# A hybrid MLA / mLSTM / MoE step on one core: w_o and x of the output stage loaded one stage earlier, into other rooms

## The reference, cut to what matters

```python
xp = layer_norm(ALPHA_RES * xp + gp1 * mixer_out(o_p, h_p, mo_p, p), p['ln1_g'], p['ln1_b'])   # mixer_out ends in @ w_o
xs = layer_norm(ALPHA_RES * xs + gs1 * mixer_out(o_s, h_s, mo_s, p), p['ln1_g'], p['ln1_b'])
u2 = concatenate([xp * (1 + scp2) + shp2, xs * (1 + scs2) + shs2])
logits = u2 @ router_w + router_b            # top 4 of 32 experts, softmax over the 4
f = moe(u2)                                  # w_up (32, 1024, 2048), w_down (32, 1024, 1024)
xp, xs = layer_norm(ALPHA_RES * x + g2 * f)  # ln2
```

## Time and profile before

| what | value |
|---|---|
| median of 3 runs (lowest, highest) | 2225.05 us (2221.8, 2225.31) |
| the profiled execution: time / span in the trace | 2224.97 us / 2223.1 us |
| PE busy, share of the span | 1879.3 us, 85% |
| decode attention (508.0 to 664.3 us) | 156.3 us, PE busy 142.10, DMA 39 GB/s |
| output and router (664.3 to 821.4 us) | 157.1 us, PE busy 119.17, DMA 212 GB/s |
| experts (821.4 to 2151.0 us) | 1329.6 us, PE busy 1127.29, DMA 319 GB/s |
| combine (2151.0 to 2223.0 us) | 72.0 us, PE busy 50.67, DMA 182 GB/s |

### The profile page before, as it was taken

One profiled execution on the slowest core, in us unless ns is written; L12 is line 12 of the kernel. 1 busy time (PEld: TensorE's weight loads), 2 busy tenths in 40 slices (PEclk: granted clock), 3 DMA queues, 4 the chain that ended last, 5 costly groups with the idle time before them and its releaser, 6 DMA issues. The chain is left out here.

```text
span 2223.1 us, 52280 instructions
## 1 busy us (share of the span) xinstructions
PE 1879.3 (85%) x21217; PEld 1085.7 (49%) x21218; DVE 606.0 (27%) x1916; ACT 443.0 (20%) x1005; POOL 206.9 (9%) x277
## 2 busy tenths in 40 slices
PE   4999897988986959999758998497797969999947
PEld 2546485566563545555324554153354535555523
DVE  2412255163332552222101221021121212222215
ACT  0102112322210012222211222021122212222210
POOL 0000101100001200011000110000000000110125
PEclk9998958898987969999978999698899979999978
DMA  9342114400309178089999089999989996651884
GB/s 361 136 154 86 47 57 159 137 1 24 85 6 290 57 307 354 24 334 409 404 402 385 24 331 410 402 402 409 401 310 403 402 410 251 241 231 42 344 317 155
DMA packets 170208, 539.49 MB, mean 243 GB/s; under 512 B 26202, under 2 KB 75550, under 8 KB 137396
## 3 DMA queue, kind: packets, MB, share of 16 engines
q1 hardware_dynamic: 143744, 502.33, 58.8%
q0 software_dynamic: 7392, 22.81, 3.0%
q10 hardware_dynamic: 19028, 13.77, 2.1%
HBM read 504.73 MB, written 33.99 MB: 242 GB/s over the span
## 5 line engine op out<-in xcount | busy, mean ns | idle before, releaser
L1697 PE MATMUL psum<-arena 128*32 128x256 f32 x11904 | 733.0, 399 | 151.3 <-DMA arena<-in_w_up 131.3
L1697 PEld LDWEIGHTS psum<-arena 128*32 128x32 f32 x11904 | 392.8, 115 | 446.5 <-DMA arena<-in_w_up 158.9
L1706 PE MATMUL psum<-arena 128*32 128x256 f32 x5952 | 357.5, 381 | 30.3 <-DMA arena<-in_w_down 15.8
L1749 DVE TENSOR_TENSOR arena<-psum,arena 128x256 f32<-128x256 f32 x186 | 79.0, 425 | 1017.0 <-PE psum L1697 1017.0
L1706 PEld LDWEIGHTS psum<-arena 128*32 128x32 f32 x5952 | 187.4, 110 | 161.0 <-issue 23.2
L1670 ACT ACT_TABLE_LOAD x93 | 119.3, 1283 | 211.6 <-issue 211.6
L1670 ACT ACTIVATE arena<-arena 128x128 f32<-128x128 f32 x186 | 57.7, 310 | 380.1 <-DVE arena L1753 380.0
L406 PE MATMUL psum<-arena 128*128 128x512 f32 (+2 forms) x400 | 128.6, 480 | 0.0
L1641 POOL COPY arena<-arena 128x1 uint32 (+1 forms) x94 | 17.0, 181 | 1133.6 <-PE psum L1687 1114.1
L1672 ACT ACTIVATE arena<-psum 128x128 f32<-128x128 f32 x186 | 51.6, 277 | 246.0 <-PE psum L1692 246.0
L406 PEld LDWEIGHTS psum<-arena 128*128 128x128 f32 x400 | 70.6, 209 | 58.0 <-issue 58.0
(11 more groups left out here) (347 smaller groups left out, 1666.8 us busy)
## 6 DMA issues: line engine op xcount, KB each, us to landing
arena<-in_w_up SPq DMA_DIRECT2D x128, 2048.0 KB, 20.7
arena<-in_w_down SPq DMA_DIRECT2D x64, 2048.0 KB, 29.8
arena<-in_w_ada SPq DMA_DIRECT2D x10, 2048.0 KB, 17.5
d_y<-arena ACTq DMA_DIRECT2D x372, 32.0 KB, 5.2
arena<-in_w_in SPq DMA_DIRECT2D x5, 2048.0 KB, 8.1
d_y<-arena SPq DMA_DIRECT2D x1, 10240.0 KB, 33.1
arena<-in_cache_ckv SPq DMA_DIRECT2D x8, 1024.0 KB, 5.7
arena<-in_b_up SPq DMA_DIRECT2D x128, 64.0 KB, 13.1
```

Source lines behind the costliest of these rows:

```text
L1697: ins = pe.matmul(bank[c * U:(c + 1) * U, 0:256].rearrange("p (g n) -> p g n", g=2), xT[:, 2 * q + k, :], up[par][q][:, k, :, c * 256 + h ...
L1706: ins = pe.matmul(Y[c * U:(c + 1) * U, 0:256], hidT[:, h, n * U:(n + 1) * U], down[par][h][:, n, c * 256:(c + 1) * 256], start=(h == 0 and ...
L1749: dve.tensor_tensor(pre, bank[:, 0:256].rearrange("p (g n) -> p g n", g=2), bu[par][:, :, h * P:(h + 1) * P], ALU.add).then_inc(s["h_sum"], 1)
```

## The change

In the decode attention stage SP gets four more DMAs, behind the eight of the new keys and ahead of the caches: w_o's first half, its second half (after `new_in`, the landing of the new keys), and x in two parts (after `ql_acc` and `ql_out`, when the latent queries are done). w_o goes to column 3000 and x to 15064, which nothing uses any more then. The output stage takes both from there and no longer loads them. The rooms left free there take u2 and x1 (36076, 38124); `tmp`, two buffers for the gated product in norm, becomes one, `tm`, at 51436. The first four rooms of `RING_AT[0]` change their order. Expert 0's w_up piece 0 is still loaded at once, piece 1 now after all transposes of the mixed rows (`mT_acc`), pieces 2 and 3 after the last project as before. The last four loads of the stage (w_down of expert 0, two pieces of expert 1) now stand behind the waits for the stores of x1 and u2 and for the transposes of u2 (`uT2_acc`). The instructions of PE, DVE, ACT and POOL and their waits are the same.

```diff
-RING_AT = [[3000, 7096, 27576, 31672, 35768, 39864], [43960, 48056, 11192, 15288, 19384, 23480]]
+RING_AT = [[31672, 27576, 3000, 7096, 35768, 39864], [43960, 48056, 11192, 15288, 19384, 23480]]
...
+    v.wo, v.x_in = v.cut(3000, 2, KD, 512), v.cut(15064, NT, D)
...
+            w_o = I["w_o"][0]
+            sp.dma_start(v.wo[:, 0], w_o[:, 0:512].rearrange("(k p) n -> p k n", p=P)).then_inc(s["wo_in"], 16)
+            sp.wait_ge(s["new_in"], 16 * B)
+            sp.dma_start(v.wo[:, 1], w_o[:, 512:].rearrange("(k p) n -> p k n", p=P)).then_inc(s["wo_in"], 16)
+            sp.wait_ge(s["ql_acc"], 2 * H)
+            sp.wait_ge(s["ql_out"], 2 * H + 1)
+            sp.dma_start(v.x_in[:, 0:NP_T, :], I["x_prompt"][0].rearrange("(t p) d -> p t d", p=P)
+                         ).then_inc(s["x2_in"], 16)
+            sp.dma_start(v.x_in[:, NP_T, :], I["x_sample"].rearrange("b t d -> (b t) d")).then_inc(s["x2_in"], 16)
             sp.wait_ge(s["yz_out"], 16)
...
-    wo = v.cut(27884, 2, KD, 512)
-    x = v.cut(36076, NT, D)
+    wo, x = v.wo, v.x_in
...
-    u2 = v.cut(15064, 2, D)
-    x1 = v.cut(17112, 2, D)
-    tmp = v.cut(19160, 2, D)
+    u2 = v.cut(36076, 2, D)
+    x1 = v.cut(38124, 2, D)
+    tm = v.cut(51436, D)
...
-            for q in range(2):
+            def first(q):
                 sp.dma_start(v.cut(RING_AT[0][q], 2, 2 * FF), first_up(0, q)).then_inc(s["ring_in"][q], 16)
-            for t in range(NT):
+
+            first(0)
+            for t in range(NT):
+                if t == NT - 2:
+                    sp.wait_ge(s["mT_acc"], 2 * NT)
+                    first(1)
                 if t == NT - 1:
                     sp.wait_ge(s["wo_acc"], NT)
-                    for q in range(2, 4):
-                        sp.dma_start(v.cut(RING_AT[0][q], 2, 2 * FF), first_up(0, q)).then_inc(s["ring_in"][q], 16)
+                    first(2)
+                    first(3)
...
+            for par, n in ((0, (NT + 1) // 2), (1, NT // 2)):
+                sp.wait_ge(s["x1_out"][par], 16 * n)
+                sp.wait_ge(s["u2_out"][par], 16 * n)
+            sp.wait_ge(s["uT2_acc"], 2 * NT)
             for h in range(2):
                 sp.dma_start(v.cut(RING_AT[0][4 + h], 4, D), first_down(0, h)).then_inc(s["ring_in"][4 + h], 16)
```

More of the change, by code:

```diff
@@ L1318, in _ @@
         def _(sp):
-            for j in range(2):
-                sp.dma_start(wo[:, j], I["w_o"][0][:, j * 512:(j + 1) * 512].rearrange("(k p) n -> p k n", p=P)
-                             ).then_inc(s["wo_in"], 16)
             spread_rows(sp, G, v, 2, 3, s["G_in"])
-            sp.dma_start(x[:, 0:NP_T, :], I["x_prompt"][0].rearrange("(t p) d -> p t d", p=P)).then_inc(s["x2_in"], 16)
-            sp.dma_start(x[:, NP_T, :], I["x_sample"].rearrange("b t d -> (b t) d")).then_inc(s["x2_in"], 16)
             sp.dma_start(ln[:, 0], bcast_rows(I["ln1_g"][0], P)).then_inc(s["x2_in"], 16)
@@ L1346, in _ @@
                 sp.dma_start(v.cut(RING_AT[1][q], 2, 2 * FF), first_up(1, q)).then_inc(s["ring_in"][6 + q], 16)
-            for par, n in ((0, (NT + 1) // 2), (1, NT // 2)):
-                sp.wait_ge(s["x1_out"][par], 16 * n)
-                sp.wait_ge(s["u2_out"][par], 16 * n)
         @block.scalar
@@ L1470, in norm @@
                 dve.wait_ge(s["wo_acc"], t + 1)
-                tm = tmp[:, t % 2]
                 dve.tensor_tensor(tm, two(2 + 2 * (t % 2)), G[:, 0, who], ALU.mult).then_inc(s["wo_read"], 1)
```

## The result

The changed kernel takes 2204.9 us (median of 4 runs, 2204.43 to 2208.96), the kernel before 2224.07 (4 runs, 2221.8 to 2225.31): a ratio of 0.9919, interval 0.9902 to 0.9936, or 18 us less (19.2 between the medians). 2206.6 was forecast. In the sets of the experiments two executions (3666.82 and 7523.64 us, where the others lay between 2203 and 2236) count in none of the ratios and medians. The profiled execution took 2205.34 us for a span of 2203.5, 19.6 us under the span of before.

The account below looks back on a forecast made before the run. The output stage's load queue was taken to bound the kernel, through ln_b, norm(0) and router(0). 17.1 us for router(0) plus 1.3 for the clock made 18.4 off 2225.0: 2206.6 us, range 2202 to 2211.

Parts of the forecast that it names:

- two terms of the sum: Output stage: router(0) 17.1 us earlier, plus 1.3 us from PE's clock behind it, together 18.4 us.
- The queue, not the loads' own time, sets norm(0).: Output stage: without w_o and x in the load queue, ln_b lands sooner and norm(0) starts at 687.0, not 704.16.
- u2(0), not PE, is late next: Ahead of router(0): u2(0) is there at 700.9, PE done at 698.3, so PE waits 2.6 us.
- the term of 17.1 us: Output stage: router(0) moves from 718.03 to 700.9, 17.1 us earlier (15.6 to 18.6).
- project(0): PE in the output stage: project(0) starts at 668.15 without waiting for w_o and ends at 683.5 (682.1 to 684.9).
- The clock: PE behind router(0): a shorter wait may keep the clock up, worth 1.3 us, with 0 and 2.7 as ends.
- the clock of the other tiles: PE's other tiles in the output stage: an allowance of 1.5 us either way.
- The dip stays: Output stage's queue: the nine slow slices, mostly G's eight 16-partition DMAs, keep their measured rate of about 136 GB/s.
- The overlap in pairs: Output stage's dip: the 136 GB/s was put down to 16-partition DMAs that may overlap in pairs.
- Decode attention hides the early loads: Decode attention: the early 6.8 MB end by 534 us, 130 us before they are needed, and cost nothing.
- The deferred weights: End of output stage: the last four loads land at 818.0, before the experts at 821.43; rival of 2211.7 us, 7 in 100.
- Rival 4, the clock of the experts: Experts' stage: PE with less rest might be granted less clock; at 0.90 the kernel takes 2230 us; 4 in 100.

Follow-up runs that it names:

- e1: The changed kernel with only w_o loaded early, x again in the output stage behind the gate, shift and scale rows: ratio 0.9951, median 2212.67 us.
- e2: The changed kernel with only x loaded early, w_o again loaded at the head of the output stage: ratio 0.9947, median 2215.95 us.
- e6: The changed kernel with each of the eight gate-row DMAs writing 16 partitions 8 apart, not neighbours: 2235.18 us, one run, not comparable because values differ.
- e9: The changed kernel with four of the eight gate-row DMAs issued by ACT, the others by SP: 2200.79 us, ratio 0.9901; changed kernel 2206.12 in that set.
- e7: The changed kernel with ln1's rows on their own semaphore, awaited only before DVE multiplies by them: ratio 0.9912, median 2205.45 us.
- e3: The changed kernel with the eight gate-row DMAs issued in the order 0,4,1,5,2,6,3,7: ratio 0.9921, median 2206.78 us.
- e4: The changed kernel with the eight gate-row DMAs issued in the order 0,2,1,3,4,6,5,7, neighbours writing the same ports: 2211.77 us, one run.

## Why the prediction was right

The mechanism was right: the queue set norm(0), and u2(0) was what was late next. That the stage came within 0.3 us of the forecast is in part luck, because two terms of the sum missed by more than 1 us each, in opposite directions. Where 17.1 us were forecast for router(0) and 1.3 for the clock, the stage shows 18.3 and -0.2.

- *The queue, not the loads' own time, sets norm(0).* Forecast 687.0, measured 687.00; e1 and e2 move it by each load's bytes. x was worth 6.4 us ahead of the stage's queue (e2) and 7.5 as the last step (e1); both together took 17.4 us off DVE's wait, where 17.0 were forecast. Counted from PE's first transpose, which came 0.3 us later than before, norm(0) starts 22.3 us in, 22.6 forecast.
- *u2(0), not PE, is late next.* Forecast a wait of 2.6 us, measured 2.27. The 13.9 us from norm(0) to router(0) became 13.0: POOL's second operation for u2(0), 3.20 us before, took 2.34, and it was DVE's operation beside it that was stretched, to 2.00. The forecast had kept the 3.20. So the term of 17.1 us measured 18.3 (53.6 - 35.3): 0.9 from here and 0.3 from norm(0).
- *project(0).* Forecast to end at 683.5; the next piece starts at 682.97.
- *The clock.* 1.3 us was a middle between 0 and 2.7, and router(0) to router(1) took 21.1 us where it had taken 22.6: 1.5. The granted clock was 1.00 over the wait, 0.77 in the 1.8 us behind it and 0.50 from 701.8 to 705.4. Twelve profiles say more than the one did. With a wait of 0 (e6), 0 (e9) or 1.4 us (e2) ahead of router(0) this piece takes 19.9 to 20.0 us; with 2.2 to 3.6 us (six profiles) 21.1, 21.2, 21.5, 22.75, 22.8 and 22.8; with 5.0 to 12.0 (e7, before, e1) 22.55 to 22.8. The hope behind the middle, that a wait of 2.6 us may not reach the fall of the clock, was therefore wrong in all six, and the size was right by the luck of the middle. The clock also took 1.7 us back at project(4), 15.68 us where it took 13.98, with 0.89 granted in place of 1.00: 18.3 + 1.5 - 1.7 is the stage's 18.1. The forecast had 1.5 us either way for the clock of the other tiles, and this used all of it and a little more. No run shows what made project(4) slow: it took 15.5 to 15.7 us in six of the twelve profiles and 13.98 in the other six.
- *The dip stays.* Right, eight slices and two parts. Its mechanism was given as ports reached by DMAs that overlap in pairs. The partitions reached are what counts (e6), as the page "SBUF — State Buffer" of the Trainium skill has it in "Door 1: The DMA port swizzle"; its 104 GB/s for 16 neighbouring partitions is somewhat under the 120 to 135 seen, and its 189 for twice the ports, which by its rule 16 partitions 8 apart reach, near e6's 193 to 231. That it is the ports, and not something else that goes by partition, no run here separates. The overlap in pairs is what fell (e3, e4, the landings).
- *Decode attention hides the early loads.* w_o's halves landed at 522.2 and 527.6, x at 535.2, before the first cache was issued; the stage did not grow.
- *The deferred weights.* Forecast to land 3.4 us before the barrier, measured 3.5.
- *Rival 4, the clock of the experts,* did not come: the granted mean over that stage is 0.92 in both profiles. Its price for 0.90 was summed wrong: 0.02 x 1300 = 26 us on top of 2206.6 is 2233, not 2230.

The 1.5 us between the stage's 18.1 and the span's 19.6 are the 1.75 in the experts and combine, less the 0.25 ahead.

## What to carry to other kernels

Where a barrier separates stages, count the bytes that the next stage loads for itself. Divided by the queue's rate they were the delay of its first work here, one load after another, and rooms that were free one stage earlier, under a queue that was nearly idle, bought them back in full (17.4 us of 17.0). Then ask what is late next: here a second chain stood 2.3 us behind the first, and a wait removed there alone (e7) was paid back in contention between DVE and POOL. And the eight DMAs of 16 neighbouring partitions were slow whatever stood around them: which partitions each reached (e6), and from how many queues they came (e9), was worth more than their order (e3, e4).

## What the runs showed of the hardware

- Eight DMAs of 16 neighbouring partitions and 192 KB each moved 120 to 135 GB/s; with their partitions 8 apart, 193 to 231; from two queues, 143 to 164. The DMAs of 128 partitions around them moved some 300 to 420.
- Eight such DMAs issued 0.5 to 0.6 us apart in one queue landed one after the other, every 1.5 us (every 0.9 us with their partitions 8 apart).
- A DVE operation of two SBUF inputs took 3.46 us in place of 1.22 when it began 1.26 us into a POOL operation of 5.38 us on SBUF, and 1.23 when it began 3.96 us into it. POOL's own product took 3.20 or 3.21 us in place of 2.34 beside DVE's.
- PE's clock: a wait of 1.4 us cost nothing, waits of 2.2 to 3.6 us cost 1.2 to 2.9 us in the 20 us that followed, and longer ones, up to 12 us, no more than that. Behind the wait of 2.3 us the granted clock was 0.50 for 3.6 us; over it, 1.00.
